# Keeping the rows of the last expert block on chip in a two-layer mixture-of-experts kernel

## What is computed

```python
y_buf = lax.map(expert_block, (x_buf.reshape(NB, MOE_BLOCK, D), block_expert)).reshape(P, D)
y = jnp.sum(y_buf[dest].reshape(T, TOP_K, D) * weights[..., None].astype(h.dtype), axis=1)
...
x = x + hierarchical_moe(h, ...)
...
z = h @ w_in[i]
u_pool = z[..., :POOL_WIDTH]
q, k, v = ...
```

## Time and profile before

| what | value |
|---|---|
| median of 3 runs (lowest, highest) | 1499.66 us (1498.92, 1499.67) |
| the profiled execution's own time | 1497.15 us |
| its span, first to last instruction | 1495.4 us |
| PE busy | 1402.1 us (94%) |
| DVE busy | 957.5 us (64%) |
| ACT busy | 772.8 us (52%) |
| POOL busy | 200.6 us (13%) |
| share of PE in the chain that ended last | 72% |
| mean granted TensorE clock | 0.969 |

### The profile page before, as it was taken

The page is one execution under the profiler, slowest core; times in us unless marked ns, Lnnn a source line. Parts: engine busy times, 40 slices in busy tenths (PEclk is TensorE's granted clock), DMA queues, the critical chain, the costliest instruction groups (busy, mean ns, idle before and its releaser), DMA issues.

```text
span 1495.4 us, 19865 instructions
## 1 busy us (share of the span) xinstructions
PE 1402.1 (94%) x6629; PEld 1067.2 (71%) x6630; DVE 957.5 (64%) x1154; ACT 772.8 (52%) x963; POOL 200.6 (13%) x235
## 2 busy tenths in 40 slices
PE   7899999999799999999999994979989999999998
PEld 6787667455577777777677763746768888888886
DVE  6845443254899999999998977385644422443185
ACT  4333434123689999999888873344133311342031
POOL 1021001000222122222211220042100000000010
PEclk8999999999999999999999995999989999999999
DMA  6131114306699999999999974122122332233131
GB/s 227 57 113 57 57 42 168 148 17 222 237 400 409 407 417 407 415 411 401 412 403 413 409 243 182 43 70 85 62 92 72 113 113 69 101 113 145 67 113 57
DMA packets 67894, 298.58 MB, mean 200 GB/s; under 512 B 18110, under 2 KB 20220, under 8 KB 55548
## 3 DMA queue, kind: packets, MB, share of 16 engines
q1 hardware_dynamic: 55612, 275.86, 47.7%
q10 hardware_dynamic: 6864, 13.54, 2.5%
q0 software_dynamic: 5360, 8.40, 1.7%
HBM read 292.00 MB, written 14.94 MB: 205 GB/s over the span
## 4 chain that ended last, share of the span: by engine, by line
PE 72%; DVE 6%; DMA 5%; issue 2%; ACT 2%; POOL 1%; DVEq 0%; POOLq 0%; SPq 0%; ACTq 0%
PE ps L714 13%; PE ps L899 12%; PE ps L914 12%; PE ps L752 7%; DMA ring<-in_w_gate 4%; PE ps L745 4%; PE ps L570 4%; PE ps L785 3%; PE ps L723 3%; PE ps L948 3%; PE ps L500 2%; PE ps L451 2%; PE ps L878 1%; PE ps L703 1%; PE ps L604 1%
## 5 line engine op out<-in xcount | busy, mean ns | idle before, releaser
L1997 DVE TENSOR_TENSOR ring_r<-ring,hi 128x2048 fp32r<-128x2048 f32 (+1 forms) x224 | 431.3, 1982 | 17.9 <-ACT hi L1444 15.8
L1444 ACT ACTIVATE hi<-ring 128x2048 fp32r<-128x2048 f32 (+1 forms) x224 | 363.0, 1662 | 11.4 <-DMA ring<-in_w_gate 7.3
L2034 DVE TENSOR_TENSOR ring_r<-ring,ring_two 128x2048 fp32r<-128x2048 f32 (+1 forms) x46 | 102.2, 2260 | 120.7 <-ACT ring_two L1518 120.5
L1518 ACT ACTIVATE ring_two<-ring 128x2048 fp32r<-128x2048 f32 (+1 forms) x46 | 83.9, 1867 | 142.5 <-PE ps L914 121.6
L1117 POOL TENSOR_TENSOR rsv<-msv,half 128x1 f32<-128x1 f32 (+2 forms) x32 | 39.0, 1221 | 722.3 <-DVE msv L1628 702.3
L714 PE MATMUL ps<-ring_r,XTS 128*128 128x512 f32 x512 | 128.6, 394 | 4.8 <-issue 2.5
L914 PE MATMUL ps<-ring_two,ats 128*128 128x512 f32 x512 | 126.6, 389 | 0.0
L714 PE MATMUL ps<-hi,XTS 128*128 128x512 f32 x512 | 126.5, 389 | 0.0
L500 PE MATMUL ps<-ring_r,ring_r 128*128 128x512 f32 x448 | 117.8, 413 | 7.6 <-DVE M L1693 4.5
L752 PE MATMUL ps<-hi,HIDS 128*64 128x512 f32 x512 | 122.9, 392 | 0.0
L714 PEld LDWEIGHTS ps<-ring_r,XTS 128*128 128x128 f32 x512 | 96.9, 190 | 28.2 <-issue 5.8
(11 more groups left out here) (322 smaller groups left out, 2145.2 us busy)
## 6 DMA issues: line engine op xcount, KB each, us to landing
ring<-in_w_up SPq DMA_DIRECT2D x32, 2048.0 KB, 17.1
ring<-in_w_gate SPq DMA_DIRECT2D x32, 2048.0 KB, 14.8
ring<-in_w_down SPq DMA_DIRECT2D x32, 2048.0 KB, 15.8
ring<-in_w_ff SPq DMA_DIRECT2D x16, 2048.0 KB, 8.2
ring<-in_w_in SPq DMA_DIRECT2D x8, 2048.0 KB, 8.0
ring<-in_w_out SPq DMA_DIRECT2D x2, 2048.0 KB
ring<-in_w_ple_gate SPq DMA_DIRECT2D x2, 2048.0 KB
X<-in_x ACTq DMA_DIRECT2D x4, 512.0 KB, 5.0
```

The lines of the kernel that those rows point to most:

```text
L1444: act.activation(HI[u][:, c], ring[:, s, c], ACT.Copy).then_inc(w_hi, 1)
L1518: act.activation(hi_of(u, a, part_size(u)), ring[:, s, a:a + part_size(u)], ACT.Copy).then_inc(w2_hi, 1)
L1997: vec.tensor_tensor(ring_r[s][:, c], ring[:, s, c], HI[u][:, c].bitcast(F32), ALU.subtract).then_inc(w_lo, 1)
L2034: vec.tensor_tensor(ring_r[s][:, a:a + n], ring[:, s, a:a + n], hi_of(u, a, n).bitcast(F32), ALU.subtract).then_inc(w2_lo, 1)
```

## The change

The rows of the last expert block no longer go through DRAM. Its result is copied out of PSUM with each row multiplied by its weight (`slot_last[:, 0:1]`), as a high part YWH on ACT and a low part YWL on DVE. S01 is a matrix of 64 slots by 512 tokens that holds a one where the slot belongs to the token. PE multiplies YWH and YWL with S01, which spreads the rows over the tokens. `results` is filled with zeros at the start of the kernel, so that the rows of the last block, never scattered, add nothing; the other blocks' results are loaded while the last block computes. The transposed x of the second layer arises in PSUM as a sum: YWH times S01, the tiles of X times the identity, YWL times S01. X itself gets the last block's rows later, in attention steps 0 to 2 (`last_rows`, `rows_added`).

For this, more moves:

- POOL fills a 128x2048 tile with zeros ahead of its first roots and issues four DMAs of 1 MB after them.
- A new product "last" (weight and token of each slot of the last block) stands on PE behind `extra(7)`, and ACT waits for it ahead of part 5 of the first expert's weights.
- SP loads `results` behind `q2` and ahead of `kv2`, into ring slots 5 and 4. `kv2` goes to the second half of slot 1, `mix0` to slot 5.
- ACT splits `q2` within the last block: half 0 ahead of the copy of the gate result, half 1 ahead of that of the up result. DVE does half 0 in the block, half 1 after the four tiles.
- `q2` 0 comes ahead of `kv2` 0; half (2,1) of `pool2` moves two steps ahead.

```diff
@@ build, routing and projections on PE
+            pe.wait_ge(last_hot, 1)
+            o = open_turn(pe, "last", 5)
+            for j in range(2 * TT):
+                ins = pe.matmul(o[0:BLK, 0:2], POS1H[:, j, :], LASTV[:, j, :], start=(j == 0), stop=(j == 2 * TT - 1))
+            fill_turn(ins, "last")
...
+            def from_last(v, k, start, stop):
+                return pe.matmul(ps[:, X3_BANKS[k], :], v[:, k // 4, k % 4 * P:(k % 4 + 1) * P], S01, start=start, stop=stop)
+
+            def from_sums(t, k):
+                pe.matmul(ps[:, X3_BANKS[k], t * P:(t + 1) * P], X[:, t, k * P:(k + 1) * P], ident[:, :], start=False, stop=False)
...
-                for c in range(2):
-                    transposes(("x3", t, c), 2 + (2 * t + c) % 4, X[:, t, c * 512:(c + 1) * 512], 4)
+                for k in range(DT):
+                    from_sums(t, k)
+            pe.wait_ge(x3_ready, TT)
+            pe.wait_ge(yw_lo, 2)
+            for k in range(DT):
+                from_sums(TT - 1, k)
+                fill_turn(from_last(YWL, k, False, True), ("x3", k))
+
+            def last_rows(r):
+
+                t, c = divmod(r, 2)
+                o = open_turn(pe, ("xr", r), jobs[0] % 2)
+                jobs[0] += 1
+                for n, v in enumerate((YWH, YWL)):
+                    ins = pe.matmul(o, S01[:, t * P:(t + 1) * P], v[:, c, :], start=(n == 0), stop=(n == 1))
+                fill_turn(ins, ("xr", r))
@@ SP
+                elif u == "kv2":
+                    sp.wait_ge(results_in, 1)
+                    for t in range(TT):
+                        for k in range(2):
+                            sp.dma_start(YG[k][:, t, :], results[k * T + t * P:k * T + (t + 1) * P, :]).then_inc(yg_in[t], 16)
+                    freed(NE - 1, 1)
...
+                elif u == "mix0":
+                    sp.wait_ge(x3_ready, TT)
@@ POOL
+            pool.memset(ZEROS, 0.0).then_inc(zero_set, 1)
...
+            for part in results.rearrange("(a p b) d -> a p (b d)", a=TT, p=P):
+                pool.dma_start(part, ZEROS).then_inc(zeroed, 16)
...
+                if ahead is None:
+                    until(pool, y_out, g * 16 + 16)
+                    pool.memset(BEGUN, 0.0).then_inc(results_in, 1)
+                    return
@@ ACT
+                if ahead is None:
+                    act.wait_ge(gate_raw_used, g + 1)
+                    part_hi(0, 0)
                 gate_or_up(0)
...
+                if ahead is None:
+                    part_hi(0, 1)
                 gate_or_up(1)
...
+                if ahead is None:
+                    for c in range(2):
+                        act.wait_ge(y_full, g * 2 + (c + 1))
+                        act.activation(YWH[:, c, :], ps[0:BLK, 4 + c, :], ACT.Copy, scale=slot_last[:, 0:1]).then_inc(yw_hi, 1)
+                    return
...
                 if part == 5:
                     filled(act, "slots")
                     act.wait_ge(wts_ready, 1)
+                    filled(act, "last")
...
-                if n in (3, 7, 9):
-                    part_hi(*{3: (2, 1), 7: (3, 0), 9: (3, 1)}[n])
+                if n in (1, 7, 9):
+                    part_hi(*{1: (2, 1), 7: (3, 0), 9: (3, 1)}[n])
@@ DVE
+                if t == 1:
+                    last_lo()
+            part_lo(0, 1)
...
+            def rows_added(r):
+                x = X[:, r // 2, r % 2 * 512:(r % 2 + 1) * 512]
+                leave(vec.tensor_tensor(x, x, filled(vec, ("xr", r)), ALU.add), ("xr", r))
...
+                for r in ROWS_AT.get(n, ()):
+                    rows_added(r)
```

More of the change, by code:

```diff
@@ L735, in expert_block @@
                 summed(1)
-                turn_rows(g + 1)
+                if ahead is not None:
+                    turn_rows(g + 1)
                 until(pe, y_left, g * 2 + 1)
```

199 lines of the change are left out of this document (115 added, 84 removed).

## The result

The changed kernel takes 1507.0 us (median of 8 runs, 1504.17 to 1512.35); the kernel before 1498.38 (8 runs, 1496.45 to 1499.67). The ratio is 1.0058, 95% interval [1.0046, 1.0071]: the change makes the kernel slower by 0.6%. The forecast was 1494.0 with a range up to 1500.5, and the time lies above it. The profiled execution took 1506.49 us, with a span of 1504.5, where that of before took 1497.15 and 1495.4, so what is to be explained is 9.1 us of span.

What follows compares the result with a forecast made beforehand. It took full DMA engines to bound the expert loop, and a chain of latencies the stretch after the last block. Terms -9.2 + 3.3 + 0.2 = -5.7 us on the median 1499.66 gave 1494.0 us, range 1487.0 to 1500.5.

Steps and rivals of the forecast that it cites:

- The start: Kernel start: zeros delay the first weights' load little, covered by ACT's later wait of 2.36 us; +0.2 us, bounds 0 and 2.
- "last": Ahead of the expert loop: ACT's part 5 waits for this product, so the first expert product starts 3.3 us later.
- The loop: Expert loop: a later start is carried through, since back-to-back loads can't catch up; no change of its own length.
- The last block: Last expert block: ACT waits for q2, so products slip 4.0 us, and a clock dip of some 3 us costs 1.5.
- The handover: Last block's end to the 72 products: scatter, load and alternating DVE and PE work go; -17.6 us.
- tile 3's pairs: Handover, behind the fourth tile: eight pairs of a float32 and a YWL product, 8 x (0.235 + 0.228) = 3.7 us.
- Rival D: Handover: plain float32 products cost four times a transpose, 0.54 us each; +4.5 us, 1504.2; chance 0.03.
- Attention: Attention: pool2's split, low parts and row products' bank turns delay the early steps; 5.9 us of the gain given back.
- the credit of 3.3 us in step 4: Attention: without PE's pool2 wait, step 3's to step 5's `biased` takes 6.7 us instead of 9.95.
- A: Loop start and last block: one or both new stalls absent; 1490.7, or 1486.7 with q2 in time; chance 0.22.
- B: Attention and loop start: bank turns cost 9 instead of 5.9, the loop's shift is 5; 1498.8; chance 0.18.
- C: From the last block on: the clock stays at 1.2 GHz; +10.5 us, 1510.2; chance 0.07.

Runs made afterwards that it cites:

- fill_late: The changed kernel, but POOL issues the fill of zeros only after the three first weight units have landed; 1.0016 times the kernel before, 6.3 us less than the changed kernel.
- fill_only: The kernel before, with only the fill of the results with zeros added at the start; 1.0031 times the kernel before, +4.6 us.
- q2_behind: The changed kernel, but ACT splits q2 after the last block's hidden copies, DVE's low parts after the four tiles; 1.0024 times the kernel before.
- no_rows: The changed kernel without the last block's row products and their additions in attention steps 0 to 2; 0.9984 times the kernel before, 11.1 us less than the changed kernel.
- rows_banks: The changed kernel, with row products on PSUM banks 7, 5 and 6 and ahead of the step's piece; 0.9999 times the kernel before.
- all_six: The changed kernel with late fill, earlier "last", earlier first-row copy, q2 behind copies, YWL behind tile 1, rows moved, pool2 inside step 0; 0.9938 times the kernel before.
- all_better: The kernel with six edits, plus ACT's last extra copy ahead of the first gathered rows and PE opening late banks later; 0.9902 times the kernel before, 1482.7 us.

## Why the prediction was wrong, point by point

**The start: +5.9, predicted +0.2.** This is the step that failed first. The prediction put the end of the first weights' load 2 to 3 us behind the start of the zeros and let ACT's 2.36 us at the earlier trace rows cover the rest. It asked when the first unit lands and not the others. The second unit's last megabytes share the 16 DMA engines with 4 MB of zeros, which is 10 us at 400 GB/s, and ACT's split of it starts 6.7 us late; ACT's wait for PE in the earlier trace rows then covers nothing, as its next instruction waits for that load. The bounds, 0 and 2, didn't hold it. The rows were there: the zeros' size, and a DMA share near 1 until 26 us. The Trainium skill (DMA: Bandwidth & Descriptors, Issuing engines are not separate DMA queues) says that DMAs issued by different engines run on the same 16 DMA engines and interleave. The split's wait of 6.64 us agrees.

**"last": +2.5, predicted +3.3.** Right in mechanism and in size.

**The loop: -0.3.** It carries a shift, as read from the earlier trace rows; `fill_late` and `fill_only` confirm it from both sides.

**The last block: +8.7, predicted +5.5.** The mechanism was right, and `q2_behind` shows that the whole slip hangs on it. The size was off in both terms in this profile. The up copy stands 14.11 us behind the block's first product; in `q2_behind` 7.57 (898.90 against 891.33). That is 6.5 instead of 4.0. `q2` was in 24.1 us after SP's issue, where the reading of the earlier trace rows gave 23.0, and SP issued it 14.1 us ahead of the block's first product instead of 15.9. The remaining 2.2 is the clock, for which I had 1.5: by the windows it was at half from about 901 to 911 us, and not for 3. Part of this miss is chance: in the ten other profiles with the same block the up copy stands 10.4 to 13.7 us behind the block's first product, so 2.9 to 6.2 late, with the prediction's 4.0 inside, and the whole stage costs 5.3 to 8.2. What none of them bears out is the dip of 3 us: the clock was at half for 6.8 to 10.3 us in each.

**The handover: -14.4, predicted -17.6.** The tiles took what was predicted (DVE ends 6.5 us behind PE's last product, predicted 7.2), and the load cost nothing. The term that failed is tile 3's pairs, 0.463 us a pair by the rows of either kind, 0.85 in fact (about 6.7 us for the eight and not 3.7): the rows priced each kind among its like, and not the change between them. Besides, PE came to tile 3 at 922.1, 0.9 us behind DVE's last addition, since it wasn't through with the other tiles; by the prediction's own terms this would be 0.5 (905.3 + 24 x 0.235 = 910.9), and it had nothing. Rival D was wrong: plain float32 held its 0.234 us. The 1.75 in the prediction is a slip of reading: the earlier trace rows has four plain float32 products in 1.05 us and eight transposes in 1.07, a factor of two. The Trainium skill (TensorE: Matmul & The Clock Gate, Terms) states a factor of four for float32; at 128 columns this trace shows two.

**Attention: +9.3, predicted +5.9.** Up to step 3 the prediction held. The second scores are 2.2 us later than before the change, relative to the first, the third another 3.3, the fourth 0.8; 3.0, 3.1 and 1.0 were predicted. At DVE's `biased(3)` the loss is 9.05 us (974.87 - 945.32 against 966.05 - 945.55), where the prediction's terms give 9.15. The chain of step 1 is there in the trace: `pool2`'s half 0, DVE's low part, the exponentials, ACT's copy of `q2` 1, and the row product that waits 0.94 us for it; `no_rows` shows only that nobody else is held up by it.

What failed is the credit of 3.3 us in step 4. PE's wait of 2.36 us for (2,1) is gone, as predicted. But step 3's scores are now so late, behind DVE's additions and (2,1), that PE waits 2.82 us for the turned scores in step 4 instead of 0.89, and behind that wait the clock is at 0.50. The fourteen instructions from 979.34 to 982.96 take 3.62 us, and their like behind them, at full clock, 2.08 (four in 0.93, two in 0.55, eight in 0.60), which makes 1.5 us. From `biased(3)` to `biased(5)` it is 8.89 us against 9.95 before: 1.1 given back instead of 3.3. With the rows on their own banks and ahead of the piece (`rows_banks`), neither the long wait nor this fall is there.

By the turned scores of step 5, which come 38.3 us after the first scores against 30.3, the loss is 8.0. Another 1.3 comes later. From 1038 to 1040 us the changed kernel computes at a granted clock of 0.50, PE busy all the time, and from 1031 to 1033, the same place before, it was 1.00; between the turned scores at 1036 and PE's products at 1078 the loss grows by 1.2 us, from 7.4 to 8.6. The rest I can't name.

**The rivals.** The forecast, A and B held 0.90, and none of them has the start in it; C had +10.5, but for a clock that stays down through the handover, and it came back at 911 us, 3.5 ahead of the handover's first product, after 10 us at half clock. The time came out near C's by another road, which is luck. Four errors of 3 to 6 us to the same side (start, last block, handover, attention) made the 14.8 us between -5.7 and +9.1.

## What to carry to other kernels

A large DMA that nothing waits for is not free while anything else is landing: look for the last load under way at that time, not the first, and put the new one behind it. A product or an addition that is slipped between two steps of a tight pipeline costs by what queues behind it, on its engine and on its PSUM bank; put it where both engines are waiting under a long piece, on a bank of its own. And a price from a row of like instructions holds only in such a row: the same products in turns with another kind, on another number of rows, took almost twice as long.

## What the runs showed of the hardware

- Products in turns, one with 64 rows and one with 128, took 0.42 us each at full clock, where each kind in a row takes 0.234 (128 columns, plain float32) and 0.26 (512 columns, float32r). The bank and the type were ruled out by runs, type and columns by a row of the kernel before. A change of rows costs 0.2 us.
- A plain float32 product of 128 columns by an identity took 0.234 us here, about twice a transpose, and one of 512 columns and 64 rows about 1.06 in turns.
- PE's way into the expert loop takes 2.5 to 2.9 us in which it computes nothing. In `all_six` PE waits ahead of the loop for ACT's copy of the last extra product, which ends at 386.47. The low parts that PE's first product needs are there at 385.85 (weights) and 386.70 (rows), and it comes at 389.33, 2.86 us behind the copy. In `all_better` that copy is early, and the product comes 2.49 us behind PE's last transpose:

```profile
387.71 3.44 PE L743 MATMUL ps<-ring_r,XTS 128*128 128x512 f32 x8 [2.49 <-issue]
```

DVE's low part, which this product reads, was there at 386.58, 1.1 us ahead of it. In the changed kernel the product comes 0.40 us behind the low part (394.74), so there the way in is hidden behind that wait. What PE spends the time on the trace doesn't show; the kernel has register loads and a branch there.
